# Gated attention on one core: high parts of 18 weight units made by ScalarE instead of GpSimd

## What is computed

```python
h = rmsnorm(x, norm_mix[l])
proj = h @ w_in[l]
q, k, v, r, lr_f, lr_b, u, g_a, g_b = jnp.split(proj, split_points, axis=-1)
...
log_a_f = jax.nn.log_sigmoid((lr_f @ w_decay_up_fwd[l] + b_decay_fwd[l]).astype(jnp.float32)) / GATE_NORMALIZER
log_a_b = jax.nn.log_sigmoid((lr_b @ w_decay_up_bwd[l] + b_decay_bwd[l]).astype(jnp.float32)) / GATE_NORMALIZER
...
o_fwd = gla_chunked(qh, kh, vh, af, include_diag=True)
o_bwd = jnp.flip(gla_chunked(jnp.flip(qh, 2), jnp.flip(kh, 2), jnp.flip(vh, 2), jnp.flip(ab, 2),
                             include_diag=False), 2)
o = o_fwd + o_bwd
o = o * lax.rsqrt(jnp.mean(o * o, axis=-1, keepdims=True) + EPS)
```

## Time and profile before

| | us |
|---|---|
| median of 3 runs | 2720.55 (2720.12 to 2721.54) |
| the profiled execution's own time | 2718.93 |
| its span on the core | 2717.2 |
| TensorE busy in the span | 2603.9 (96%) |
| ScalarE busy | 1043.1 (38%) |
| GpSimd busy | 1240.1 (46%) |
| VectorE busy | 1865.4 (69%) |

### The profile page before, as it was taken

How to read it: one execution, slowest core, us unless ns; L and a number is a source line. 1 busy time by engine, 2 the same in 40 slices (tenths; PEclk the granted TensorE clock), 3 DMA queues, 4 the chain that set the end, 5 groups by cost and what they waited for, 6 DMA issues and landing times.

```text
span 2717.2 us, 32442 instructions
## 1 busy us (share of the span) xinstructions
PE 2603.9 (96%) x12370; PEld 2098.1 (77%) x12370; DVE 1865.4 (69%) x2116; ACT 1043.1 (38%) x1450; POOL 1240.1 (46%) x769
## 2 busy tenths in 40 slices
PE   6999999999999999999998999989898999999998
PEld 5788778877777888887876788656786888877777
DVE  6656655556758766668879647666558766777887
ACT  5222443333224333334435211666455333434444
POOL 3322222223436888885333433241034988823331
PEclk9999999999999999999999999999999999999999
DMA  4334233334342332346642343401323545654543
GB/s 164 121 98 123 93 124 100 118 116 148 132 147 86 101 114 78 115 130 199 214 135 55 129 151 101 124 1 46 117 83 96 170 133 167 206 162 157 169 140 140
DMA packets 335776, 339.81 MB, mean 125 GB/s; under 512 B 18667, under 2 KB 254806, under 8 KB 335622
## 3 DMA queue, kind: packets, MB, share of 16 engines
q1 hardware_dynamic: 329654, 315.19, 37.2%
q10 hardware_dynamic: 5968, 22.55, 2.1%
HBM read 228.88 MB, written 107.77 MB: 124 GB/s over the span
## 4 chain that ended last, share of the span: by engine, by line
PE 52%; DVE 9%; issue 2%; ACT 2%; DMA 1%; POOL 1%; SPq 0%; DVEq 0%; ACTq 0%; POOLq 0%
PE ps L3617 36%; PE ps L568 8%; DVE op_lo L3694 2%; PE ps L2690 2%; PE ps L2713 1%; DVE sw_lo L3527 1%; PE ps L2700 1%; PE ps L3193 1%; DVE acc L3938 1%; DVE acc L3945 1%; DVE acc L2216 0%; DVE x L2637 0%; DMA x_block<-acc 0%; DVE op_lo L3597 0%; PE ps L3578 0%
## 5 line engine op out<-in xcount | busy, mean ns | idle before, releaser
L3617 PE MATMUL ps<-op_hi,sw_hi 128*128 128x512 f32 x1769 | 691.8, 391 | 15.9 <-DVE op_lo L3694 8.6
L3617 PE MATMUL ps<-op_hi,sw_lo 128*128 128x512 f32 x1769 | 688.4, 389 | 0.0
L3617 PE MATMUL ps<-op_lo,sw_hi 128*128 128x512 f32 x1769 | 688.4, 389 | 0.0
L3617 PEld LDWEIGHTS ps<-op_hi,sw_hi 128*128 128x128 f32 x1769 | 332.0, 188 | 96.5 <-issue 17.2
L3617 PEld LDWEIGHTS ps<-op_hi,sw_lo 128*128 128x128 f32 x1769 | 332.0, 188 | 69.6
L3617 PEld LDWEIGHTS ps<-op_lo,sw_hi 128*128 128x128 f32 x1769 | 332.1, 188 | 68.6 <-issue 0.5
L534 POOL TENSOR_TENSOR w_hi_t<-w_raw,ones 128x1024 fp32r<-128x1024 f32 (+1 forms) x60 | 117.0, 1954 | 535.7 <-DMA w_raw<-in_w_in 244.7
L3517 ACT ACTIVATE sw_hi<-sw_sumNone 128x512 fp32r<-128x512 f32 (+1 forms) x252 | 157.1, 624 | 330.1 <-PE ps L3617 246.5
L3527 POOL TENSOR_TENSOR sw_lo<-sw_sumNone,sw_hi 128x512 fp32r<-128x512 f32 x138 | 214.5, 1564 | 33.7 <-ACT sw_hi L3517 33.6
L3478 POOL TENSOR_TENSOR sw_sumNone<-sw_raw 128x512 f32<-128x512 f32 (+1 forms) x63 | 114.1, 1810 | 230.8 <-DVE sw_lo L3527 199.3
L3517 ACT ACTIVATE sw_hi<-sw_raw 128x512 fp32r<-128x512 f32 (+1 forms) x189 | 117.5, 622 | 198.1 <-PE ps L3617 196.3
(11 more groups left out here) (477 smaller groups left out, 5471.7 us busy)
## 6 DMA issues: line engine op xcount, KB each, us to landing
op_raw<-hidden SPq DMA_DIRECT2D x42, 1024.0 KB, 8.7
w_raw<-in_w_in SPq DMA_DIRECT2D x47, 512.0 KB, 4.6
sw_raw<-in_w_ffn_in SPq DMA_DIRECT2D x44, 512.0 KB, 5.3
hidden<-hidden_blocks SPq DMA_DIRECT2D x13, 1536.0 KB, 6.2
hidden<-hidden_blocks SPq DMA_DIRECT2D x14, 1280.0 KB, 5.0
sw_raw<-in_w_up SPq DMA_DIRECT2D x32, 512.0 KB, 8.5
sw_raw<-in_w_down SPq DMA_DIRECT2D x32, 512.0 KB, 5.3
acc<-proj SPq DMA_DIRECT2D x30, 512.0 KB, 4.6
```

The source lines that it names most:

```text
L3617: mm = pe.matmul(out, w, x[:, k, :], start=(k == 0 and i == 0 and r < 4), stop=(k == n - 1 and i == 2), skip_group_check=r >= 4)
```

## The change

For units 3 to 20, ScalarE makes the high part, with a Copy of 128 x 1024 (`split_hi`, which was there for other stages), and GpSimd keeps the low part (`split_lo`). Units 1 and 2 are split by GpSimd alone as before. A new helper `unit_hi(h, i)` waits for `w_split` (the split of the unit before), then for `w_landed` (the tile) and `unit_done` (the buffers), and copies. It is called at five fixed places in each head of ScalarE's order.

```diff
@@ mid_pool
                 if u < MID0 + 2:
                     pool.wait_ge(S["in_product"], N_IN_SEQ - 2 if u == MID0 else N_IN_SEQ)
-                split_unit(pool, Step(u))
+                    split_unit(pool, Step(u))
+                else:
+                    split_lo(pool, Step(u))
@@ gla_act
+            def unit_hi(h, i):
+                if (h, i) == (0, 1):
+                    return
+                u = Step(MID0 + MIDS * h + i)
+                act.wait_ge(S["w_split"], u.c)
+                split_hi(act, u)
+
...
                         act.activation(Ering[m % 2], src[:, :], ACT.Exp, scale=scale).then_inc(S["e_ready"], 1)
                         if h and d == 0 and i == 1:
                             store_o(h - 1)
+                            unit_hi(h, 1)
...
                     if d == 0:
+                        unit_hi(h, 2)
                         act.wait_ge(S["sc_ready"], n + 1)
...
                         act.activation(sct[:, :, :], PS[1][:, :].rearrange("p (c s) -> p c s", c=C), ACT.Copy)\
                            .then_inc(S["sc_fwd"], 1)
+                    if d == 1:
+                        unit_hi(h, 3)
                     act.wait_ge(S["kdt_ready"], n + 1)
...
                     act.activation(kdtok[:, :, :], PS[2][:, :].rearrange("p (c s) -> p c s", c=C), ACT.Copy)\
                        .then_inc(S["kdtok_ready"], 1)
+                unit_hi(h, 4)
                 if h < GH - 1:
                     gate_log(h + 1, 0)
                 for e in range(2):
                     act.wait_ge(S["o_ready"], 2 * h + e + 1)
                     act.activation((qs if e == 0 else ks)[:, :], PS[1 + e][:, :], ACT.Square)\
                        .then_inc(S["osq_ready"], 1)
+                if h < GH - 1:
+                    unit_hi(h + 1, 0)
```

## The result

| | before | changed |
|---|---|---|
| median of the runs | 2721.05 us (4 runs) | 2753.06 us (2749.00 to 2754.73, 4 runs) |
| profiled execution | 2718.93 us | 2752.34 us |
| span | 2717.2 us | 2750.6 us |
| TensorE's mean granted clock | 0.991 | 0.982 |

The changed kernel is slower: ratio 1.0107, 95% interval [1.0095, 1.0119]. Between the two profiled executions lie 33.4 us.

What follows compares the result with a forecast made beforehand. The prediction took TensorE's own instruction order to bound the heads' stage. Stalls of 17.0 us plus 8.8 us of low clock made 25.8 us, forecasting 2746.4 us from 2720.55; own range 2741 to 2752, 8-in-10 range 2736 to 2754.

Steps and rivals of the forecast that it cites:

- the wide one: Range meant to hold 8 in 10, 2736 to 2754 us for the whole kernel.
- about 6: Heads' stage: each head was to take about 6 us longer in the changed profile.
- at most 1.4 us: Heads' stage: work taken off GpSimd gives back at most what VectorE's `ks` costs TensorE, 1.4 us.
- x = 1.4 us: Heads 1 to 3: `ks`, evacuation of unit (h, 0) and load of unit (h, 2) come 1.4 us earlier; other end 0.
- Four of the five places cost 0: ScalarE's copies of units (h, 3), (h, 4), (h + 1, 0) cost 0; that of (h, 1) was counted in x.
- The stall of unit (h, 2): ScalarE's copy ahead of `sct` waits for its tile, delaying z: 5.3 us in head 0, 3.9 in others, 17.0 in all.
- The clock, 2.2 us a head, 8.8 us in all: TensorE's clock falls behind each head's gap, costing 2.2 us a head, 8.8 us; ends 0 and 11.6.
- The estimate from the Trainium skill: Clock loss per stall by the skill's page: 0.8 us, not 2.2, sum near 20 instead of 26 us; not adopted.
- The first (clock holds): Rival: the stall ahead of `sct` is there but TensorE's clock holds; 2737.6 us, chance 0.13.
- The second: Rival: stall without relief, late landing in head 0, 2.9 us clock loss per gap; 2754.7 us, chance 0.17.
- The third: Rival: the copy of unit (h, 2) finds its tile landed, so not slower; 2722.0 us, chance 0.04.
- fourth: Rival: only the relief shows, everything else hides; time falls by up to 1.4 us and more, 2719; chance 0.02.

Runs made afterwards that it cites:

- late2: Changed kernel with the copy of unit (h, 2) moved behind the gate of direction 1 instead of ahead of `sct`: 2718.98 us, ratio 0.9989.
- without2: Changed kernel, but GpSimd splits unit (h, 2) of each head whole and ScalarE makes the other 14 high parts: 2719.70 us, ratio 0.9989.
- ahead_gate: late2 with the copy of unit (h, 2) one step earlier, behind `kdtok` and ahead of the gate of direction 1: 2723.84 us, ratio 1.0006.
- filled: Changed kernel with 21 extra matmuls in head 0 and 16 in the others while TensorE would wait for `sct`: 2741.43 us, ratio 1.0072.
- dense_after: Changed kernel with 10 matmuls of 512 columns behind the gap, between the wait for `sct` and z: 2758.89 us, ratio 1.0129.
- waitonly: Kernel before, plus a ScalarE wait ahead of `sct` for the tile of unit (h, 2), no copy: 2755.38 us, ratio 1.0120.
- halffill: As filled, with 13 and 8 extra matmuls instead of 21 and 16: 2753.12 us, ratio 1.0113.
- copyonly: late2 plus a second copy of unit (h, 1)'s high part, already landed, ahead of `sct`: 2718.50 us, ratio 0.9989.
- only2: Changed kernel, but ScalarE makes only the high part of unit (h, 2); GpSimd splits the other 16 units whole: 2757.70 us, ratio 1.0131.

## Why the prediction was right, and where it was off

It was right in sign, in mechanism and in place: 2746.4 us with a range of 2736 to 2754, measured 2753.06. The size was too small: 25.8 us were forecast and 32 us came between the medians. The result lies above the forecast's own range of 2741 to 2752 and 0.9 us inside the wide one, and one of the four executions, 2754.73, is outside that too. Each head took 7.4 to 10.6 us longer, not about 6. Point by point:

- *TensorE bounds the stage, and taking work off GpSimd gives back at most 1.4 us there.* TensorE does bound the stage, and its waits for `ks` in heads 1 to 3 are gone. But "at most 1.4 us" was too low. late2 and without2 won 0.11%, about 3 us, and a part of that is the wait for `kd`, which I had left out (kernel before, 285 to 645 us):

```profile
PE ps L1243 <- DVE kd L1479: 0.9, 4, 0.2
```

In late2's profile the evacuations of unit (1, 0) and (2, 0) lie 87.2 us apart, 479.66 - 392.47 by SyncE's stores, against 482.12 - 394.07 = 88.05 us before, so 0.9 us a head in three heads.
- *ks comes x = 1.4 us earlier.* From the evacuation of unit (0, 4) to the start of `ks` the changed kernel takes 399.35 - 387.51 = 11.84 us, the one before 391.69 - 378.26 = 13.43. That is 1.6. The rows, the first of the changed kernel, the other two of the one before:

```profile
387.51 1.23 DVE L676 TENSOR_TENSOR stage<-ps,rstd 128x1024 f32<-128x1024 f32 x1 [6.92 <-PE ps L568]
```
```profile
378.26 1.23 DVE L676 TENSOR_TENSOR stage<-ps,rstd 128x1024 f32<-128x1024 f32 x1 [6.92 <-PE ps L568]
...
391.69 1.21 DVE L1471 TENSOR_TENSOR ks<-acc,lt 128x1024 f32<-128x1024 f32 x1
```

- *Four of the five places cost 0.* Right: without2.
- *The stall of unit (h, 2).* I had 17.0 us, and z came 16.6 us later in all. That the sum is so close is luck, since two errors cancel: head 0 lost 6.7 us and not 5.3, heads 1 to 3 lost 3.2 to 3.3 us each and not 3.9. In heads 1 to 3 the relief was 1.6 us instead of 1.4, the tile came after 4.7 us instead of 4.8, and `sct` followed the copy without a gap. In head 0 I held that GpSimd had started late because of VectorE and put the landing at 311.2. In the changed kernel, with ScalarE waiting instead, the tile came 6.5 us after the issue, in ahead_gate 6.1 us, as GpSimd's 6.1 us had said. Head 0's visible gap is only 5.4 us, since the low clock had already stretched the scores and transposes ahead of it by 1.3 us.
- *The clock, 2.2 us a head, 8.8 us in all.* **This is the term that was mis-sized.** From z's start to unit (h, 1) head 1 took 417.74 - 408.83 = 8.91 us, before 401.10 - 396.25 = 4.85 us: 4.1 us a head, 16.3 us over the four in the profiled execution. filled gave 14.6 us of it back in its profiled execution and 11.6 us in medians. I had averaged the losses behind four gaps elsewhere in the kernel, behind which the clock was low for 3 to 6 of 8 us; here it stayed low through all 8. What follows differs (there, in three of four, 512-column matmuls, here z's 32-row ones and the 256-column ones of keys times values), but dense_after does not show that this is the reason. My upper bound from the same rows, 2.9 us each, was too low as well.
- *The estimate from the Trainium skill*, TensorE: Matmul & The Clock Gate, section "HAM oscillation", 0.8 us a stall, was further off than the rows of the trace. What that section tells of its kernel in words, that the clock falls again at every wait of 3 to 5 us, agrees with the trace: it fell behind all four gaps of 4.3 to 5.4 us.
- *ScalarE's queue is first in, first out*, as the Trainium skill has it in TensorE: Matmul & The Clock Gate, section "Architectural detail". The trace agrees: nothing passed the waiting copy, `sct` stood behind it while it waited for 3.9 to 6.2 us, and waitonly shows the same with a bare wait.
- *The rivals.* The first (clock holds) is what filled makes by force: 2741, against 2737.6 by my sum. The second (no relief, late landing, 2.9 us a gap: 2754.7) is closest to the measured time, and its late landing in head 0 came true, but the rest are other terms: the relief was there, the clock was dearer still. The third and fourth fell.

## What to carry to other kernels

When a step is moved into another engine's fixed order, its own microsecond is the small part: compare the issue of what it waits for with the time the engine gets there, and price the wait by the instructions behind it. A wait of 4 to 6 us in each head in front of `sct` cost 32 us in all, one step later 5 us, two steps later nothing, for the same work. When the wait opens a gap in TensorE's work, price the matmuls behind the gap at both clocks: here the low clock doubled the bill, 16.3 us behind 16.6 us of delay.

## What the runs showed of the hardware

- The clock's fall behind a gap is not set by the gap's length alone. The 2.7 us gap ahead of the scores of head 0 is in every profile; in those of the changed kernel, waitonly, halffill and copyonly the scores behind it ran slow (2.99, 3.02, 2.97 and 3.64 us), in the other eight at full speed (2.05 us in the kernel before, only2, filled and late2).
- Behind the four gaps of 4.3 to 5.4 us of the changed kernel, followed by z and keys times values, the clock stayed at 1.2 GHz for all of the next 8 us; in only2, behind gaps of 4.8 to 6.0 us, for 6.4 to 8 of the 8 us (mean clock 0.50, 0.54, 0.60, 0.50). Behind the four gaps of the kernel before it was low for about 3 to 6 of the 8 us.
- In filled the clock fell in head 3, some 2 us after z began, behind 3.9 us of extra matmuls and an open rest of 0.76 us; in heads 1 and 2, with the same filling and rests of 0.70 and 0.79 us, it did not.
- A wait on a DMA can be booked as "issue" in the list of waits: 18.0 us ahead of L544 in the changed kernel, 18.8 us named as DMA in waitonly at the same place.
- A load of the same size took 5.9 to 6.5 us from issue to its user's start in head 0 and 4.6 to 4.9 us in heads 1 and 2, in all ten profiles in which an engine stood waiting for it. In head 3 it took 4.6 to 4.9 us in eight of them and 6.25 and 6.14 us in halffill and dense_after. Why was not tried.
